# Expert gather with normalised rows loaded 32 tokens at a time, six row buffers, and its loops written out

## The reference, cut to what matters

```
idx, gate = product_keys(h @ wq, keys)     # 128 experts and 128 softmax weights a token
a = gelu(sum(u[idx] * h, -1))              # u[idx]: 128 rows of 2048, gathered
y = (gate * a) @ v[idx]                    # v[idx]: 128 rows of 2048
out = rmsnorm(x + mod * y, final)
```

## Time and profile before

| | us |
|---|---|
| median of 3 runs | 3269.28 |
| lowest, highest | 3259.94, 3271.04 |
| the profiled execution's own time | 3268.68 |
| its span, first to last instruction | 3266.7 |
| busy in the span: PE, DVE, ACT, POOL | 3062.3, 2397.7, 1894.9, 334.7 |
| read from memory | 781.55 MB |

### The profile page before, as it was taken

The page is one execution under the profiler, slowest core; times in us unless marked ns, Lnnn a source line. Parts: engine busy times, 40 slices in busy tenths (PEclk is TensorE's granted clock), DMA queues, the critical chain, the costliest instruction groups (busy, mean ns, idle before and its releaser), DMA issues.

```text
span 3266.7 us, 44841 instructions
## 1 busy us (share of the span) xinstructions
PE 3062.3 (94%) x12354; PEld 2131.3 (65%) x12354; DVE 2397.7 (73%) x4371; ACT 1894.9 (58%) x4174; POOL 334.7 (10%) x444
## 2 busy tenths in 40 slices
PE   8999999999999999988987799899999999999998
PEld 6777878888787877766775222222222788888886
DVE  6787776788767567866858899988888555555556
ACT  5555545555556765454454577777777555555555
POOL 1000000000000000000000333333333000000001
PEclk9999999999999999988999555555555899999999
DMA  7666666776666657950843799999999655555553
GB/s 251 206 206 206 213 226 219 237 253 232 226 219 227 180 162 260 351 206 14 300 133 117 310 385 388 352 370 380 380 358 381 230 189 189 190 191 192 193 193 142
DMA packets 213731, 788.43 MB, mean 241 GB/s; under 512 B 17730, under 2 KB 18450, under 8 KB 151522
## 3 DMA queue, kind: packets, MB, share of 16 engines
q1 hardware_dynamic: 158864, 406.89, 36.9%
q0 software_dynamic: 51344, 370.53, 30.2%
q10 hardware_dynamic: 3396, 9.43, 0.8%
HBM read 781.55 MB, written 5.24 MB: 241 GB/s over the span
## 4 chain that ended last, share of the span: by engine, by line
PE 58%; DVE 16%; DMA 15%; ACT 5%; issue 4%; DVEq 2%; ACTq 0%; POOLq 0%; POOL 0%; SPq 0%
DMA u_ring<-in_peer_u,idx 12%; PE bank L538 10%; PE bank L540 10%; PE bank L539 10%; PE bank L2786 7%; PE bank L2788 7%; PE bank L2787 7%; DVE u_ring L2606 5%; DVE w_lo L529 3%; DVE acc L593 2%; ACT w_hi L525 2%; DMA raw<-in_w_in 1%; PE bank L2518 1%; DMA ada_ring<-in_ada_w 1%; ACT prob L920 1%
## 5 line engine op out<-in xcount | busy, mean ns | idle before, releaser
L525 ACT ACTIVATE w_hi<-raw 128x512 fp32r<-128x512 f32 x1008 | 621.6, 630 | 664.8 <-PE bank L540 585.2
L529 DVE TENSOR_TENSOR w_lo<-raw,w_hi 128x512 fp32r<-128x512 f32 x1008 | 667.3, 692 | 340.0 <-ACT w_hi L525 335.6
L538 PE MATMUL bank<-w_hi,xt_hi 128*128 128x512 f32 x1632 | 660.0, 404 | 40.8 <-DVE w_lo L529 40.5
L2606 DVE CUSTOM_DVE_ANT_0 u_ring<-u_ring,bank 128x1024 f32<-128x1024 f32 x512 | 604.6, 1218 | 86.4 <-DMA u_ring<-in_peer_u,idx 62.7
L539 PE MATMUL bank<-w_lo,xt_hi 128*128 128x512 f32 x1632 | 638.7, 391 | 0.0
L540 PE MATMUL bank<-w_hi,xt_lo 128*128 128x512 f32 x1632 | 638.5, 391 | 0.0
L2518 PE MATMUL bank<-row_ring,three 3*128 3x512 bf16 x1024 | 512.2, 616 | 46.4 <-DVE act_in L2606 30.2
L2705 DVE TENSOR_TENSOR w_lo<-v_raw,w_hi 128x512 fp32r<-128x512 f32 x496 | 343.3, 693 | 278.3 <-ACT w_hi L2678 277.3
L2678 ACT ACTIVATE w_hi<-v_raw 128x512 fp32r<-128x512 f32 x496 | 313.2, 632 | 313.4 <-PE bank L2788 313.4
L2786 PE MATMUL bank<-w_hi,vw_hi 128*128 128x512 f32 x992 | 391.7, 395 | 2.8 <-DVE w_lo L2705 2.8
L538 PEld LDWEIGHTS bank<-w_hi,xt_hi 128*128 128x128 f32 x1632 | 307.9, 189 | 125.5 <-DVE w_lo L529 51.1
(11 more groups left out here) (449 smaller groups left out, 3285.3 us busy)
## 6 DMA issues: line engine op xcount, KB each, us to landing
v_raw<-in_peer_v SPq DMA_DIRECT2D x128, 1024.0 KB, 4.8
ada_ring<-in_ada_w POOLq DMA_DIRECT2D x96, 1024.0 KB, 6.0
raw<-in_w_in_ab SPq DMA_DIRECT2D x128, 512.0 KB, 4.0
raw<-in_w_in_c SPq DMA_DIRECT2D x128, 512.0 KB, 4.4
raw<-in_w_in SPq DMA_DIRECT2D x120, 512.0 KB, 4.5
raw<-in_w_out_ab SPq DMA_DIRECT2D x32, 512.0 KB, 4.7
raw<-in_w_out_c SPq DMA_DIRECT2D x32, 512.0 KB, 5.5
raw<-in_w_out SPq DMA_DIRECT2D x32, 512.0 KB, 6.9
```

Of the source, the lines that this page charges most:

```text
L525: act.activation(w_hi[:, s % WS, :], raw[:, q % RAW, s % KC, :], ACT.Copy).then_inc(hi_ready, 1)
L529: dve.tensor_tensor(w_lo[:, s % WS, :], raw[:, s // KC % RAW, s % KC, :], w_hi[:, s % WS, :].bitcast(F32), ALU.subtract).then_inc(raw_used, 1)
L538: pe.matmul(o, a_hi, b_hi, start=kk == 0, stop=False, skip_group_check=True)
L2606: dve.tensor_tensor_reduce(u, u, bank[:, 2 * hf:2 * hf + 2, :].rearrange("p b n -> p (b n)"), 1.0, 0.0, ALU.mult, ALU.add, (act_in, act_ha ...
```

## The change

Six buffers for u's rows: four in u_ring as before, two more (u_more) in the place of x. ACT stores x to memory (x_rows) behind the three parts, POOL waits for that store, and SP loads x back behind the first four blocks of the values stage; the last additions wait for it. SP loads the parts of 32 tokens at a time, three DMAs of 32 rows each into 96 partitions of row_ring, two such groups in turn. PE's weights for the spread are a column of one_row, 96 rows that are 1 at the token's place in each of the three parts and 0 elsewhere, repeated over 128 columns by a step of zero. POOL takes the indices from idx itself. All loops of the gather are written out, and the sem_inc and register steps that went with them are gone. The choice of the second half is taken at other places: gate_exp_act before token 112 (104 before), gate_dve behind token 119, choose_turn_pe before the row of token 122 (before token 114's), take_choice_dve behind token 127.

```diff
+RING = 6
+BATCH = 32
+        x_rows = nc.dram_tensor("x_rows", (S, D), F32, kind="Internal").ap()
-        three = const("three", [P, P], BF16)
-        idx4 = [const(f"idx4{i}", [P, 4], U32) for i in range(2)]
+        one_row = const("one_row", [P, BATCH], BF16)
+        u_more = at("u_more", [P, 2, D], X_AT)
...
             act.dma_start(count128[:, :], A["count128"]).then_inc(keys_landed, 16)
+            act.dma_start(x_rows.rearrange("(t p) d -> p t d", p=P), x[:, :, :]).then_inc(x_saved, 16)
...
             gate_dve(dve, 0)
-            dve.memset(three[:, :], 1.0)
+            dve.tensor_tensor(one_row[:, :], eye[:, 0:BATCH], eye[:, BATCH:2 * BATCH], ALU.add)
+            dve.drain()
+            dve.tensor_tensor(one_row[:, :], one_row[:, :], eye[:, 2 * BATCH:3 * BATCH], ALU.add)
             take_choice_dve(dve, 0)
...
+        GATE_AT, TURN_AT = 112, 120
+        def u_slot(n):
+            return u_ring[:, n % RING, :] if n % RING < 4 else u_more[:, n % RING - 4, :]
+        def read(n):
+            return 2 * PRE + 2 * n + 2
         def experts_pool(pool):
...
+            pool.wait_ge(x_saved, 16)
+            for n in range(S):
+                if n % P == 0:
+                    pool.wait_ge(idx_ready, n // P + 1)
+                if n >= RING:
+                    pool.wait_ge(halves_read, read(n - RING))
+                pool.indirect_dma_start(u_slot(n), None, A["peer_u_2"][0],
+                                        bass.IndirectOffsetOnAxis(ap=idx[:, n:n + 1], axis=0)).then_inc(u_landed[n % RING], 16)
...
+            for g in range(S // BATCH):
+                if g >= 2:
+                    sp.wait_ge(half_spread, 2 * PRE + 2 * BATCH * (g - 1))
+                for i in range(3):
+                    sp.dma_start(row_ring[BATCH * i:BATCH * (i + 1), g % 2, :], hf_rows[i, BATCH * g:BATCH * (g + 1), :]).then_inc(rows_landed[g % 2], 16)
...
-                        last = pe.matmul(bank[:, 2 * hf + b, :], three[k:k + 3, :], rows_slot(j)[:, c:c + 512], start=True, stop=True)
+                        last = pe.matmul(bank[:, 2 * hf + b, :], wide(one_row[0:3 * BATCH, i:i + 1], [3 * BATCH, P]),
+                                         row_ring[0:3 * BATCH, g % 2, c:c + 512], start=True, stop=True)
...
+            for n in range(S):
+                dot(n)
+                if n < P:
                     next(later, None)
-                    if j % 4 == 3:
+                    if n % 4 == 3:
                         next(later, None)
...
-                if m == GATE_PASS:
+                if n == GATE_AT + 7:
                     gate_dve(dve, 1)
-                if m == TURN_PASS:
+                if n == TURN_AT + 7:
                     take_choice_dve(dve, 1)
...
             four(0, True)
+            sp.wait_ge(x_saved, 16)
+            sp.dma_start(x[:, :, :], x_rows.rearrange("(t p) d -> p t d", p=P)).then_inc(x_back, 16)
...
             passes_of_blocks(dve, four)
+            dve.wait_ge(x_back, 16)
```

More of the change, by code:

```diff
@@ L2499, in experts_sp, with row @@
             sp.wait_ge(rings_free, 1)
[L2500 to L2506, removed]
+            for g in range(S // BATCH):
[3 more added lines that the diff above has]
+                    sp.dma_start(row_ring[BATCH * i:BATCH * (i + 1), g % 2, :], hf_rows[i, BATCH * g:BATCH * (g + 1), :]).then_inc(rows_landed[g % 2], 16)
         def experts_pe(pe):
-            def row(m, j):
-                n = TOK * m + j
-                pe.wait_ge(rows_landed[j % 4], 16 * (2 * m + j // 4 + 1))
+            def row(n):
+                g, i = n // BATCH, n % BATCH
+                if i == 0:
+                    pe.wait_ge(rows_landed[g % 2], 48 * (g // 2 + 1))
                 for hf in range(2):
@@ L2525, in place @@
                 pe.wait_ge(one_hot, PRE + n + 1)
-                pe.matmul(bank[:, 4 + j // 4, (j % 4) * P:(j % 4 + 1) * P], hot_side1[:, j % 4, :], hot_side0[:, j % 4, :],
+                pe.matmul(bank[:, 4 + n // 4 % 2, (n % 4) * P:(n % 4 + 1) * P], hot_side1[:, n % 4, :], hot_side0[:, n % 4, :],
                           start=True, stop=True).then_inc(placed, 1)
[L2529 to L2542, removed]
+            row(0)
+            row(1)
+            for n in range(S):
+                if n == TURN_AT:
+                    choose_turn_pe(pe, 1)
+                if n + 2 < S:
+                    row(n + 2)
+                place(n)
@@ L2562, in mark, with weigh @@
[L2562 to L2566, removed]
+                act.activation(hot_side1[:, n % 4, :], apart[:, n % 2, 1, :], ACT.Relu, scale=neg_gate_t[:, at_], bias=gate_t[:, at_])
+                act.activation(hot_side0[:, n % 4, :], apart[:, n % 2, 0, :], ACT.Relu, scale=-1.0, bias=1.0)
+            def weigh(n):
+                j = n % 8
+                act.wait_ge(halves_read, read(n))
@@ L2567, in weigh @@
                 act.activation(act_out[:, j:j + 1], act_in[:, j:j + 1], ACT.Gelu_apprx_tanh, bias=act_half[:, j:j + 1])
                 act.drain()
[L2569 to L2580, removed]
@@ L2582, in experts_act @@
-            half = PASSES // T
-            act.wait_ge(idx_ready, 1)
[L2584 to L2590, removed]
-            act.wait_ge(idx_ready, 2)
-            tokens(half - 1, 0, 0)
-            tokens(half, 1, 0)
-            with act.Fori(0, half - 2) as i:
-                tokens(i + (half + 1), 1, 1)
@@ L2596, in experts_act @@
-            tokens(PASSES - 1, 1, 1, TOK)
-            take(2 * PASSES - 1, T - 1, 1)
+                act.activation(hot_side0[:, n % 4, :], hot_side0[:, n % 4, :], ACT.Copy, scale=act_out[:, j:j + 1]).then_inc(one_hot, 1)
+            act.wait_ge(idx_ready, 1)
+            mark(0)
+            for n in range(S):
+                if n == GATE_AT:
+                    gate_exp_act(act, 1)
+                if n + 1 == P:
+                    act.wait_ge(idx_ready, 2)
+                if n + 1 < S:
+                    mark(n + 1)
+                weigh(n)
+                if n % 4 == 1 and n > 4:
+                    take(n // 4 - 1)
@@ L2609, in experts_dve @@
             later = choose_later_dve(dve)
-            half = PASSES // T
-            for m in range(half):
-                for j in range(TOK):
-                    dot(m, j)
+            for n in range(S):
+                dot(n)
+                if n < P:
                     next(later, None)
-                    if j % 4 == 3:
+                    if n % 4 == 3:
                         next(later, None)
-                if m == GATE_PASS - 1:
+                if n == GATE_AT - 1:
                     for _ in later:
                         raise AssertionError("the choice of the second half is still going on")
-                if m == GATE_PASS:
+                if n == GATE_AT + 7:
                     gate_dve(dve, 1)
-                if m == TURN_PASS:
+                if n == TURN_AT + 7:
                     take_choice_dve(dve, 1)
-            with dve.Fori(0, PASSES - half) as i:
-                for j in range(TOK):
-                    dot(i + half, j)
         LAST = [(0, 0), (1, 0), (2, 0), (0, 1), (3, 0), (1, 1), (2, 1), (3, 1)] + [(j, c) for c in (2, 3) for j in range(4)]
```

59 lines of the change are left out of this document (18 added, 41 removed).

## The result

The changed kernel takes 3223.82 us (median of 4 runs, 3221.11 to 3226.35), the kernel before 3268.35 beside it: 44.5 us less between the medians. The ratio over the runs is 0.9856, 95% interval 0.9838 to 0.9874 (the medians alone give 0.9864). The forecast was 15.0 us less with a range down to 3238: the direction holds, the size is three times what was forecast.

The account below looks back on a forecast made before the run. The prediction took the gather's DMA to set the pace, at 2.77 to 2.84 us a token, with PE close behind. Its terms, -23.6 + 1.1 + 6.9 - 1.2 + 1.0 + 0.8, gave -15.0 us: 3254 us, range 3238 to 3272.

Parts of the forecast that it names:

- The ring: Gather: six buffers in place of four keep the DMA queue filled, 386 GB/s in place of 373, -23.6 us.
- Rows by 32 tokens: Gather's row loads: same bytes in fewer loads, never waited for after the first, so 0.
- PE: Spread matmul with 96 rows in place of 3: as many matmuls and columns, clock taken to stay at 0.50, 0 us.
- The rival that saw PE slowed by the 96 rows: PE in the gather: weight loads of 96 rows may not overlap the row matmuls; +160 us, 3429 us, chance 0.06.
- The seam: Between tokens 127 and 128: POOL's load waits for DVE's later second choice, leaving the DMA idle, +6.9 us.
- The DVE stretch: 2040 to 2100, where DVE sets the pace: 6.5 us lost, two more buffers give back 5.4, +1.1 us stays.
- Small terms: POOL's index copies gone, -1.2 us; x's store to memory, +1.0; code of the written-out loops, +0.8.
- The memory's rate as a rival: Gather: 373 GB/s is what memory gives these 8 KB rows, so deeper queues gain nothing; 3271 to 3276 us, chance 0.28.

Follow-up runs that it names:

- e10: Changed kernel with four buffers, each token's row loaded by itself (three rows) and the second choice eight tokens earlier: 3263.40 us, 0.9978 of the kernel before.
- e3: Changed kernel with four buffers in place of six and each token's row loaded by itself (three rows): 3269.26 us, 1.0000 of the kernel before.
- e2: Changed kernel with each token's row loaded and spread by itself (three rows), six buffers kept: 3268.62 us, 0.9997 of the kernel before.
- e1: Changed kernel with four buffers for u's rows in place of six: 3240.55 us, 0.9902 of the kernel before.
- e5: Changed kernel plus 256 loads by SP that nobody reads, each three rows of 4 KB: 3278.03 us, 1.0013 of the kernel before.
- e14: Changed kernel with rows loaded 16 tokens at a time, 48 rows of weights in the spread: 3247.26 us, 0.9947 of the kernel before.
- e15: Changed kernel with rows loaded 16 tokens at a time, but 96 rows of weights in the spread: 3235.73 us, 0.9899 of the kernel before.
- e4: Changed kernel with the choice of the second half eight tokens earlier on all engines: 3217.97 us, 0.9844 of the kernel before.
- e9: Changed kernel with the second choice eight tokens earlier, run again with more rounds: 3215.43 us, 0.9851 of the kernel before.

## Why the prediction was wrong

In stage time the change adds up step by step: 721.9 before; written-out loops 717.2 (e10); late choice 722.0 (e3); six buffers 724.2 (e2); rows and weights 678.0. In another order the parts differ: with rows by 32 tokens the ring is worth 11.5 (e1), and rows and weights, with four buffers, 32.5 (722.0 less 689.5). That the kernel came out faster, as forecast, is luck: the part that was to bring it gave nothing by itself, and the two parts that did were put at 0.

- **The ring, -23.6.** This is the step that failed first: "I take it that the queue then stays filled as it is from 1880 to 2040", with the ring's depth as what leaves engines idle. Depth was not the limit. Six buffers alone gave nothing (722.0 in e3, 724.2 in e2); they are worth 11.5 only once the row loads are even (e1).
- **Rows by 32 tokens, 0.** "They were never waited for after the first one, so nothing goes", and "What the row loads cost the other transfers is in the 386 GB/s". It was, and that was the error: the 386 was read as the rate of a filled queue, when it was the rate beside three-row loads. The change takes them away. e5 prices them at 54 us when added, e2 with PE's part at 46 when put back.
- **PE, 0.** "As many matmuls of as many columns" holds, and the clock stayed at 0.50 as taken, but for the seam. Missing was that the 96 rows shorten the placing beside them. The 2.65 us of PE "still fit under the DMA's 2.75", but not under the 2.57 us that a token takes in the changed kernel from 2200 to 2400 (311 row matmuls, four a token). e14, with even loads and 48 rows of weights, takes 2.63 there (304) and is 18.4 us of stage behind; 96 rows give back 9.3 of them (e15). Neither part gives the whole gain by itself. The rival that saw PE slowed by the 96 rows pointed the wrong way: 111 ns a load, overlapped, and a shorter token.
- **The seam, +6.9.** Right in place and nearly in size. Timeline of the changed kernel, DVE behind token 127, POOL's load for 128, DVE's first half of 128:

```profile
2161.82 0.29 DVE L2426 CAST idx<-bank 128x128 uint32<-128x128 f32 x1
...
2163.20 0.93 POOL L2494 DMA_INDIRECT u_ring<-in_peer_u,idx  x1 [15.49 <-DVEq L2431]
...
2168.63 1.22 DVE L2582 CUSTOM_DVE_ANT_0 u_ring<-u_ring,bank 128x1024 f32<-128x1024 f32 x1 [5.74 <-DMA u_ring<-in_peer_u,idx]
```

  2168.63 - 2161.82 = 6.8 us is DVE's hole, which the prediction put at 7.3. Its 6.9 is idle time of the DMA, and what that costs the stage is read from e4 and e9: 9.0.
- **The DVE stretch, +1.1.** 352 GB/s in place of 344: two more buffers hardly help there. What the stretch moved takes 51.5 us at 410 GB/s, so by this estimate 8.5 us are lost, not 1.1.
- **Small terms.** POOL's first load is issued 2.0 us after DVE begins to write idx, 2.73 before: 0.7 us, not 1.2. Before, the copy began 1.49 us behind that write; now the load itself comes 2.0 behind it.

```profile
1807.70 0.29 DVE L2426 CAST idx<-bank 128x128 uint32<-128x128 f32 x1 [0.66 <-PE bank L2472]
...
1809.70 0.99 POOL L2494 DMA_INDIRECT u_ring<-in_peer_u,idx  x1 [190.35 <-DVEq L2841]
```

  x costs nothing that can be seen: the longest weight load beside its store takes 9.1 us (9.2 in the earlier trace rows), the stages behind the gather 0.4 us more. The written-out loops, taken as +0.8 for their code and 0 otherwise, gained 4.7 of stage with POOL's copies gone.
- **The memory's rate as a rival** falls: 409 and 414 GB/s. The Trainium skill's 358 GB/s for one core (DMA: Bandwidth & Descriptors, Specifications) is not a limit here.

## What to carry to other kernels

A DMA share near 1.00 says that engines hold packets, not that they move what they can (0.99 at 386 GB/s, 1.01 at 409); ask how many rows each small load beside the stream has, and try 16 or 32, the counts that did well here. Where two costs lie close together, price what each becomes when the other goes: here loads by 16 tokens kept 35 of the 44 us with PE's shorter token (e15) and 25 without (e14). A rate read from a stretch of the old kernel is the rate of everything in that stretch, the part that the change removes too.

## What was not expected of the hardware

- 12 KB a token beside a 1 MB gather cost 54 us in 256 loads of three rows and 15 in 256 loads of 16 rows; beside three-row loads the gather's own packets count as longer (698 us an engine in the kernel before, 660 in the changed one), so no view shows idle engines.
- Three rows by POOL's queue cost 42 us, by SP's 54.
- A 128-row weight load of f32 is pulled ahead of matmuls that use 96 rows of weights and not of those that use 3, 12 or 48: 420 against 501 or 502 ns a placing.
- Loads of 16 rows cost 9 us more than loads of 32, with the same bytes and, by their small packets, on as many engines; why stays open.
